# GpSimd's gathers of single activations made to wait for one another in the expert down phase

## The reference

```python
a = jax.nn.gelu(jnp.einsum('td,ted->te', hb, u[e]), approximate=False)   # e: 8 x 16 experts of each position
return jnp.einsum('te,ted->td', (g * a), v[e])                           # g: their softmax gates
```

## Time and profile before

| | us |
|---|---|
| median of 3 runs | 1870.18 |
| lowest and highest run | 1859.30, 1872.53 |
| the profiled execution | 1854.62 |
| its span | 1852.5 |
| busy TensorE matmul | 1798.2 (97%) |
| busy VectorE | 1218.8 (66%) |
| busy ScalarE | 572.1 (31%) |
| busy GpSimd | 487.2 (26%) |
| software DMA queue, packets' time | 11.3% of 16 engines' span |
| hardware DMA queues of SyncE, packets' time | 41.6% of 16 engines' span |

### The profile page before, as it was taken

One profiled execution on the slowest core, in us unless ns is written; L12 is line 12 of the kernel. 1 busy time (PEld: TensorE's weight loads), 2 busy tenths in 40 slices (PEclk: granted clock), 3 DMA queues, 4 the chain that ended last, 5 costly groups with the idle time before them and its releaser, 6 DMA issues.

```text
span 1852.5 us, 31068 instructions
## 1 busy us (share of the span) xinstructions
PE 1798.2 (97%) x12753; PEld 1324.2 (71%) x12753; DVE 1218.8 (66%) x2611; ACT 572.1 (31%) x984; POOL 487.2 (26%) x515
## 2 busy tenths in 40 slices
PE   8999999989999999999999999999969999999999
PEld 6743445768888888888888888888736666566665
DVE  7558677555998983755556333444248788888885
ACT  1002134310234223444334333343213333333331
POOL 0000100000355650000000000000268778777640
PEclk9999999899999999999999999999979999999999
DMA  4422622002122333465555755555568999999991
GB/s 166 107 88 109 202 92 92 1 4 114 47 92 92 138 138 138 184 229 206 198 205 191 278 184 178 200 192 192 204 231 330 366 384 379 371 376 378 376 387 47
DMA packets 116238, 365.11 MB, mean 197 GB/s; under 512 B 12041, under 2 KB 72697, under 8 KB 104321
## 3 DMA queue, kind: packets, MB, share of 16 engines
q1 hardware_dynamic: 90416, 288.02, 41.6%
q0 software_dynamic: 25680, 75.10, 11.3%
HBM read 299.78 MB, written 63.31 MB: 196 GB/s over the span
## 4 chain that ended last, share of the span: by engine, by line
PE 87%; DVE 10%; issue 2%; ACT 1%; DMA 0%; SPq 0%; DVEq 0%; ACTq 0%
PE psum L2012 34%; PE psum L2066 27%; PE psum L1718 22%; PE psum L2033 2%; DVE u_lo L1457 1%; PE psum L1846 1%; PE psum L1724 1%; DVE rest L1384 0%; PE psum L1766 0%; PE psum L1809 0%; DVE ixs L1401 0%; DVE CI L1430 0%; DVE CI L1422 0%; DMA xT<-in_xT 0%; DVE crest L1419 0%
## 5 line engine op out<-in xcount | busy, mean ns | idle before, releaser
L2066 PE MATMUL psum<-w_hl,v_hi 128*128 128x384 bf16 x1920 | 468.0, 326 | 0.0
L2012 PE MATMUL psum<-h_hi,u_hi 128*128 128x260 bf16 x2048 | 395.1, 274 | 3.2 <-DVE u_lo L1457 2.5
L2012 PE MATMUL psum<-h_lo,u_hi 128*128 128x260 bf16 x2048 | 395.0, 274 | 0.0
L2012 PE MATMUL psum<-h_hi,u_lo 128*128 128x260 bf16 x2048 | 394.9, 274 | 0.0
L706 POOL DMA_INDIRECT trow<-in_v,t_lists x136 | 171.6, 1262 | 664.2 <-ACT act_f L916 588.1
L2066 PE MATMUL psum<-w_hl,v_lo 128*128 128x384 bf16 x960 | 313.0, 326 | 0.0
L1457 DVE TENSOR_TENSOR u_lo<-u_raw,u_hi 128x1024 bf16<-128x1024 f32 x128 | 153.9, 1217 | 209.3 <-ACT u_hi L904 209.2
L2066 PEld LDWEIGHTS psum<-w_hl,v_hi 128*128 128x128 bf16 x1920 | 187.9, 98 | 123.3 <-issue 0.2
L916 ACT ACTIVATE act_f<-psum 128x520 f32<-128x520 f32 x128 | 77.4, 605 | 465.4 <-PE psum L2012 465.4
L2012 PEld LDWEIGHTS psum<-h_hi,u_lo 128*128 128x128 bf16 x2048 | 198.7, 97 | 31.3
L2012 PEld LDWEIGHTS psum<-h_lo,u_hi 128*128 128x128 bf16 x2048 | 198.6, 97 | 31.4
(11 more groups left out here) (377 smaller groups left out, 1895.8 us busy)
## 6 DMA issues: line engine op xcount, KB each, us to landing
u_raw<-in_uT SPq DMA_DIRECT2D x32, 2048.0 KB, 9.4
v_raw<-in_v SPq DMA_DIRECT2D x32, 2048.0 KB
wr<-in_w SPq DMA_DIRECT2D x13, 2048.0 KB, 7.6
d_gate<-stage SPq DMA_DIRECT2D x12, 2048.0 KB, 8.1
d_act<-act_f SPq DMA_DIRECT2D x20, 768.0 KB, 4.5
g_in<-d_gate SPq DMA_DIRECT2D x10, 1536.0 KB
a_in<-d_act SPq DMA_DIRECT2D x20, 768.0 KB
g_up<-d_gate SPq DMA_DIRECT2D x12, 768.0 KB, 10.0
```

Of the source, the lines that this page charges most:

```text
L2012: mm = pe.matmul(upair[n % 2][:, f, 0:HALF], w[g % 2][:, k, c * P:(c + 1) * P], hs[:, k, halves[f]], start=(k == 0 and x == 0), stop=(k == ...
L2066: mm = pe.matmul(ybank[m][:, 0:DENSE], w[g % 2][:, c, m * P:(m + 1) * P], w_now[:, z, c, :], start=(g == 0 and c == 0 and x == 0), stop=(g ...
```

## The change

Each gather of activations (except the first) waits until the gather of activations ahead of it has landed. Both gathers of activations and gathers of rows are issued by GpSimd in program order, so whatever stands behind the wait stands still with it. The order is changed too: dot 0 is issued before the wait for `w_prod` and dots 1 to 7 behind it; rows 4 to 9 stand between dots 1 to 7 instead of behind dot 7; dots 8 to 15 are no longer issued ahead of row 10, but two behind each row from row 10 on, until the old distance (dot s+6 behind row s) is reached. Numbers and places of the gathers stay, as does everything on the other engines.

```diff
+ALONE = TSLOTS
...
             def slot_dot(s):
                 b = s // BATCH
                 if s % BATCH == 0 and b >= 2:
                     pool.wait_ge(t_weighed, b - 1)
+                if s >= 1 and s < ALONE:
+                    before = (s - 1) // BATCH
+                    pool.wait_ge(t_dots_in[before % 2], 16 * (BATCH * (before // 2) + (s - 1) % BATCH + 1))
                 pool.indirect_dma_start(t_dots[:, s:s + 1], None, d_acts, bass.IndirectOffsetOnAxis(
                     ap=t_arow[:, s:s + 1], axis=0)).then_inc(t_dots_in[b % 2], 16)
...
-            for s in range(BATCH):
+            slot_dot(0)
+            pool.wait_ge(w_prod, NEARLY)
+            for s in range(1, BATCH):
                 slot_dot(s)
-            pool.wait_ge(w_prod, NEARLY)
-            for s in range(4, TROWS):
-                slot_row(s)
-            for s in range(BATCH, 2 * BATCH):
-                slot_dot(s)
+                if s + 3 < TROWS:
+                    slot_row(s + 3)
+            dots = BATCH
             for s in range(TROWS, TSLOTS):
                 slot_row(s)
-                if s + 2 * BATCH - TROWS < TSLOTS:
-                    slot_dot(s + 2 * BATCH - TROWS)
+                for _ in range(2):
+                    if dots < min(TSLOTS, s + 2 * BATCH - TROWS + 1):
+                        slot_dot(dots)
+                        dots += 1
```

## The result

The changed kernel takes **2065.58 us** (median of 4 runs, 2063.48 to 2067.70) against 1870.46 for the kernel before: ratio 1.107, 95% interval 1.103 to 1.111. The direction was forecast, the size was not: 1944 us, in a range that ended at 2035.

The account below looks back on a forecast made before the run. TensorE was taken to bound the down phase. From 1372.2 us, dot steps of 372 + 22 plus 116 us foreign traffic, then 52 and 2.1 us, gave 1936; half of a 15.6 us offset made 1944 us, range 1875 to 2035.

Parts of the forecast that it names:

- What bounds the kernel now, and where a cost would appear: Down phase is TensorE's without a gap; late slots hold VectorE, which then prepares a group late.
- the signs: GpSimd's idle time grows by over 100 us, `t_acc` waits vanish, DMA share falls to about 0.8, pace 4.0 us.
- The beginning: Dots 1 to 7 end at 1364 us, costing nothing; dots 8 to 15 come late, so VectorE is late from the first batch.
- Price of foreign traffic: SyncE's loads hold up the gathers by turns: 4.0 us a group for 27 loads, plus 8 for g_in, 116 us.
- The rival that all foreign traffic adds: All 238 us of SyncE's queue add to the chain of dots, ending at 2058 us; chance 0.06.
- a pace near 5 us: Slot pace in the down phase that would prove GpSimd's gaps hide none of the foreign traffic.
- Price without foreign traffic: A slot costs GpSimd's own 3.1 us, two dots without a row between 2.7 us; an idle queue lands a dot within 1.2.
- The forecast's estimate of some 55 us more: With 2.0 us fixed DMA cost behind the issue, a slot costs 3.5 us and the sum ends some 55 us later.
- The tail: From the last dot's landing to the end of the span: 52 us.
- TensorE's clock: Rival: clock stays low after each of 29 pauses, up to 44 us, 1988 us, less what late slots hide; chance 0.07.
- The faster rival: Gathers hold TensorE from 1343.5 to 1365.2 us; the new order gives back up to 18.6 us, 1851 us; chance 0.03.
- the runs' offset: Median of runs lay 15.6 us above the profiled run; half of that was added to the forecast.

Follow-up runs that it names:

- experiments 8 and 9: Changed kernel with one, two, four dots in flight: 2063.55, 1947.32, 1847.83 us; old order, four: 1844.83; large loads cut, two: 1862.15; loads, rows, VectorE sums cut: 1894.18.
- experiment 1: Changed kernel with its new order of gathers but without the added wait: 1846.26 us against 1835.65 for the kernel before, ratio 1.006.
- experiment 3: Changed kernel with nearly all of SyncE's large loads of the down phase cut to small parts: 1931.88 us, ratio 1.053 to the kernel before.
- small_all: Changed kernel with v_raw, a_in, w_hl and g_in loads of the down phase cut to small parts: 1931.88 us, ratio 1.053 to the kernel before.
- experiment 6: Changed kernel with rows of 1 KB instead of 4 from slot 10: 1881.93 us with large loads also cut, 1996.96 us with loads whole.
- experiment 9: Changed kernel, large loads cut: with two dots in flight 1862.15 us; with 1 KB rows and VectorE's sums cut instead 1894.18 us.
- order_only: Changed kernel with its new order of gathers but without the added wait: 1846.26 us, ratio 1.006 to the kernel before.
- old_order_flight_4: Kernel before in its old order, each dot waiting for the one four ahead, four in flight: 1844.83 us, ratio 1.004 to the kernel before.
- small_all_flight_2: Changed kernel with large loads of the down phase cut and two dots in flight: 1862.15 us, ratio 1.003 to the kernel before.
- light_dve: Changed kernel with large loads cut, rows of 1 KB, and VectorE's sums and v_lo cut to 64 of 1024 columns: 1894.18 us, ratio 1.018.
- half: Changed kernel with the added wait on dots 1 to 71 only, then none: 1966.89 us, ratio 1.057 to the kernel before.

## Why the prediction was wrong in size

- **What bounds the kernel now, and where a cost would appear**: right. TensorE's pauses come from late slots, first at batch 1, as said. The removal of the backlog was named as the mechanism, and experiments 8 and 9 bear it out. Of the signs, the idle time ahead of line 704 grew by 247 us, the waits for `t_acc` vanished, and the DMA share fell to 0.68, lower than the 0.8 named.
- **The beginning**: right in kind. The late batch 1 was forecast and costs 10 us by itself (experiment 1). Dots 1 to 7 did not end by 1364: the chain there took 34 us instead of 22 (dot 1 starts at 1340.25, dot 7 has landed at 1373.8), and slot 0 came some 3 us late. The 3.1 us step failed already here, and this term had no foreign traffic, though SyncE's queue took 45.2% of the DMA engines' time from 1340 to 1374 us.
- **Price of foreign traffic**: right in size, in part by luck. Forecast 116 us, measured 121 us in the steps (experiment 3), by loads 85 for `v_raw` (forecast 79), 44 for `a_in` and `w_hl` (29), 3 for `g_in` (8). But the 116 were worked out against a chain that needs 3.1 us a step. Against the measured 3.91, the same working gives 27 x (9.0 - 1.6 x 3.91) + 8 = 81 us: the held time of 9.0 us for 1.6 slots was too short as well. The rival that all foreign traffic adds, 2058 us, came near the measured time by number, not by mechanism: its 238 us are twice what was measured. The sign named for it, a pace near 5 us, appeared (4.88) and would have misled; only the runs without loads tell the two apart.
- **Price without foreign traffic**: this step failed. The forecast called an unloaded step GpSimd's own 3.1 us, because a dot on an idle queue lands 1.2 us behind its issue. `small_all` took 1872.1 - 1375.5 = 497 us for the 127 steps from dot 8 to dot 135, 3.91 each, where 3.1 make 394: 103 us too little. What was mis-sized is above all the landing. The row in front of the dot was put at nothing, and so was the time from the landing to the next issue; measured, the two together make the landing's side of the step 3.69 us on average and not 2.7. Of the 0.81 us above 3.1, that is 0.52. GpSimd's own 3.17 us instead of 3.1 is 0.07. Another 0.15 is an error of method: the forecast compared mean with mean, but in a chain each step takes the larger of the two anew (issues vary from 0.95 us to over 2, landings from 2.2 to 7.7), and no queue averages them. The last 0.07 is all other waits. Rows of a quarter of the bytes give back 0.41 us a step, 52 of the 103 us (experiment 6), and one more dot in flight with the same work gives a step of 3.22 us (experiment 9).
- **No upper bound there.** The forecast gave the unloaded step one value and let only the loads vary, so the range had 2035 at its top, though 3.9 us instead of 3.1 alone makes 1944 + 103 = 2047. The Trainium skill's 2.0 us of fixed cost ("DMA: Bandwidth & Descriptors", "Anatomy of one DMA — SWDGE (gpsimd) path") were put behind the end of the issue and called too long. The page's list of where the time goes begins with the dispatch and the making of the descriptors; counted so, from the start of the issue, the shortest landing of 2.2 us agrees with it. The forecast's estimate of some 55 us more with that figure, 1999 us, was nearer, but by luck: behind a row the mean landing is 2.05 us behind the end of the issue (`small_all`).
- **The tail**: 52 us forecast from dot 135's landing to the end. Measured 64.3 from its start at 1997.18, so some 61 from its landing. Its six last rows are issued behind it, and VectorE waits 6.08 us for one of them.
- **TensorE's clock**: the granted clock fell, to 0.948 on average from 0.987, and in the down phase to 0.85 (1372 to 2000 us) from 1.00 (1372 to 1800 us), so part of the stretch ran at 1.2 GHz and not at 2.4. The matmuls of line 2072 take 343 ns instead of 326 on average, 45 us more busy time, near the rival's 44. Nearly all of it is hidden under the late slots: no TensorE line stands in the chain from 1380 to 2000 us, and of the last 108 matmuls before the first transposed sum (19.39 us, 0.18 us each instead of 0.163) 1.8 us lie on the path. The Trainium skill, "TensorE: Matmul & The Clock Gate", section "Part 1: The HAM clock gate (the "warmup" mystery)", says that the throttled state is the default and that activity releases it; the trace agrees, with 0.85 where TensorE pauses and 1.00 where it doesn't.
- **The faster rival and the runs' offset**: TensorE's 21.7 us of near standstill is not in the changed kernel's profile, but nor is it in those of `order_only` and `old_order_flight_4`, where no dot waits for the one just ahead of it. The half of 15.6 us that was added for the median should have been near zero (profiled 2063.48, median 2065.58).

## What to carry to other kernels

A wait for one's own last DMA turns throughput into latency. Price such a step as the larger of issue time and landing time, step by step, and not as a mean beside a mean. Read the landing from behind the traffic that stands in front on the same queue, and add what passes from the landing to the next issue (0.26 us here). How many transfers must be in flight can't be read from one landing time, because that time grows with the number in flight (medians of 3.6, 6.3 and 9.1 us for one, two and four). It has to be tried, and depends on what else the DMA engines do: two are enough without the large loads, four with them. In the new order four make the wait free, in the old order they leave 8 us. If transfers need semaphores of their own, give each transfer in flight one, and wait K back.

## What was not expected of the hardware

**TensorE at a crawl.** In three of the seventeen profiles TensorE has stretches in which it often starts one instruction in about 0.70 us or multiples of it, waiting for nothing that the profile shows: the kernel before from 1343 to 1365 us, `small_all_flight_2` from 1546 to 1561, `light_dve` from 1452 to 1501 and again from 1576 to 1588 (pieces of TensorE's chain there: start, length, what):

```profile
1453.38 0.40 issue
1454.81 1.09 issue
1455.91 0.48 PE psum L2080
1456.63 0.49 PE psum L2080
1457.33 0.48 PE psum L2080
```

The last two kernels ran on one chip (as did `half`, whose profile has none), on which the kernel before took 1857 us instead of 1836 to 1839. The string of gathers, named in the forecast as a possible cause, isn't needed: in these two the stretches lie elsewhere. The cause is open, and so is that of the kernel before being slower on some chips.

**A dot is small, its turn is not.** It moves 512 bytes in 32 packets and lands in 2.2 us at best, but in a chain, with a row in front and full-size loads beside it, each one sets a step of 4.9 us.
